# Even-layer attention: the value product as three f32r passes on split probabilities

## The reference, cut to what matters

```
def dense_gqa(q, k, v):          # 8 query heads, 2 key/value heads, head width 64
    s = einsum(q, k) * HEAD_DIM ** -0.5
    p = softmax(s)               # latent rows see all 1280 keys, context rows the 256 context keys
    return einsum(p, v)
```

## Time and profile before

| | before |
|---|---|
| runs | 3541.65, 3556.89, 3560.44 us, median 3556.89 |
| profiled execution | 3537.79 us (span 3536.0 us) |
| mean granted clock of TensorE | 0.849 |
| PE, DVE, ACT, POOL busy over the span | 79%, 43%, 29%, 15% |
| stage `attend_even`, 540 to 1110 us | PE 483, DVE 213, ACT 186, POOL 87 us busy; clock 0.91 |

### The profile page before, as it was taken

How to read it: one execution, slowest core, us unless ns; L and a number is a source line. 1 busy time by engine, 2 the same in 40 slices (tenths; PEclk the granted TensorE clock), 3 DMA queues, 4 the chain that set the end, 5 groups by cost and what they waited for, 6 DMA issues and landing times. The chain is left out here.

```text
span 3536.0 us, 34120 instructions
## 1 busy us (share of the span) xinstructions
PE 2802.4 (79%) x11887; PEld 2084.4 (59%) x11888; DVE 1531.6 (43%) x2383; ACT 1011.4 (29%) x1342; POOL 523.6 (15%) x473
## 2 busy tenths in 40 slices
PE   8948988889893699999137875876899993799991
PEld 1126865556562588888136433766788883688780
DVE  0024555343333556556442733333333333566754
ACT  0012224323231445444111012213222220455640
POOL 0012320310112200000221001321210112100001
PEclk9979989989896799999668987995777676899995
DMA  9532113611104567764620003134101104668855
GB/s 362 211 88 71 39 57 132 220 33 48 54 27 147 179 248 264 264 221 172 250 89 18 0 24 105 36 94 97 43 30 50 47 27 147 219 217 330 309 214 208
DMA packets 241445, 476.78 MB, mean 135 GB/s; under 512 B 85133, under 2 KB 98427, under 8 KB 237212
## 3 DMA queue, kind: packets, MB, share of 16 engines
q1 hardware_dynamic: 172264, 361.56, 29.3%
q0 software_dynamic: 19248, 65.60, 5.1%
q10 hardware_dynamic: 49812, 48.03, 4.2%
HBM read 387.70 MB, written 87.45 MB: 134 GB/s over the span
## 5 line engine op out<-in xcount | busy, mean ns | idle before, releaser
L2456 DVE TENSOR_TENSOR ex_gu_lo<-mw_gu,ex_gu_hi 128x2048 fp32r<-128x2048 f32 x128 | 287.3, 2287 | 78.8 <-ACT ex_gu_hi L2376 78.8
L2376 ACT ACTIVATE ex_gu_hi<-mw_gu 128x2048 fp32r<-128x2048 f32 x128 | 237.6, 1911 | 107.7 <-DVE ex_y L2503 101.7
L181 PE MATMUL mod_acc<-mod_w,mod_sT 128*2 128x512 f32 x384 | 174.5, 618 | 22.4 <-DMA mod_w<-in_ada_w 11.9
L2044 PE MATMUL at_ps_o<-at_pT,at_v_one 128*128 128x512 f32 x336 | 182.8, 626 | 1.7 <-ACT at_pT L1824 1.7
L2534 PE MATMUL ex_ps_g<-ex_gu_hi,ex_xT_hi 128*128 128x512 f32 x408 | 169.7, 416 | 8.0 <-issue 4.8
L2534 PE MATMUL ex_ps_y<-ex_d_hi,ex_hT_hi 128*128 128x512 f32 x408 | 166.5, 408 | 9.1 <-DVE ex_d_lo L2456 7.7
L2456 DVE TENSOR_TENSOR ex_d_lo<-mw_d,ex_d_hi 128x2048 fp32r<-128x2048 f32 x64 | 143.8, 2288 | 53.4 <-ACT ex_d_hi L2376 53.4
L1824 ACT ACTIVATE at_pT<-at_ps_s 128x512 f32<-128x512 f32 x168 | 99.5, 595 | 228.9 <-PE at_ps_s L2037 228.5
L2534 PE MATMUL ex_ps_g<-ex_gu_lo,ex_xT_hi 128*128 128x512 f32 x408 | 164.5, 403 | 0.0
L2534 PE MATMUL ex_ps_g<-ex_gu_hi,ex_xT_lo 128*128 128x512 f32 x408 | 164.5, 403 | 0.0
L2534 PE MATMUL ex_ps_y<-ex_d_lo,ex_hT_hi 128*128 128x512 f32 x408 | 162.0, 397 | 0.0
(11 more groups left out here) (452 smaller groups left out, 6422.6 us busy)
## 6 DMA issues: line engine op xcount, KB each, us to landing
mw_gu<-in_moe_w_gate SPq DMA_DIRECT2D x32, 2048.0 KB, 10.5
mw_gu<-in_moe_w_up SPq DMA_DIRECT2D x32, 2048.0 KB, 15.4
mw_d<-in_moe_w_down SPq DMA_DIRECT2D x32, 2048.0 KB
mod_w<-in_ada_w SPq DMA_DIRECT2D x32, 1536.0 KB, 9.4
y_d<-ex_y ACTq DMA_DIRECT2D x51, 512.0 KB
y_d<-at_zero POOLq DMA_DIRECT2D x36, 512.0 KB, 5.0
x_d<-at_x SPq DMA_DIRECT2D x18, 512.0 KB, 2.6
co_x<-x_d SPq DMA_DIRECT2D x18, 512.0 KB, 6.4
```

Of the source, the lines that this page charges most:

```text
L181: mm = nc.tensor.matmul(acc[0:2, n, :], sT[:, i, :], w[i][:, n * 512:(n + 1) * 512], start=(i == 0), stop=(i == KD - 1))
L2044: nc.tensor.matmul(ps_o[g][:, :], v_one[:, kt, g:g + 2, :].rearrange("p a d -> p (a d)"), pT[u % 3][:, :], start=(u == plan.first[i, g]), ...
L2376: nc.scalar.activation(dst, src, ACT.Copy).then_inc(sem, 1)
L2456: sub = lambda dst, a, b, sem: nc.vector.tensor_tensor(dst, a, as_f32(b), ALU.subtract).then_inc(sem, 1)
```

## The change

The value product becomes three f32r products: lo(v) hi(p) + hi(v) hi(p) + hi(v) lo(p). `v_hi` and `v_lo` are made once. For the probabilities ACT runs the same Exp twice, once into the fp32 tile `pT` (two of them now, not three) and once, rounded, into `pT_hi`. POOL subtracts the two into `pT_lo`. PE waits for POOL (semaphore `p_ready`) before the third pass. ACT waits for POOL's subtraction of step u-2 before it writes `pT` again. The space comes from the tile of zeros, cut from 1024 to 64 columns: the DMA of zeros now reads it 16 times per row.

```diff
-        v_one = ph.sb("v_one", [P, NT, 3, HD])
+        v_hi = ph.sb("v_hi", [P, NT, 3, HD], F32R)
+        v_lo = ph.sb("v_lo", [P, NT, 3, HD], F32R)
-        pT = [ph.sb(f"pT{i}", [P, 512]) for i in range(3)]
+        pT = [ph.sb(f"pT{i}", [P, 512]) for i in range(2)]
+        pT_hi = [ph.sb(f"pT_hi{i}", [P, 512], F32R) for i in range(3)]
+        pT_lo = [ph.sb(f"pT_lo{i}", [P, 512], F32R) for i in range(3)]
-        zero = ph.sb("zero", [P, D])
+        zero = ph.sb("zero", [P, D // 16])
...
 ACT, scores:
+                        if u >= 2:
+                            act.wait_ge(S["p_ready"], u - 1)
                         if u >= 3:
                             act.wait_ge(S["valued"], u - 2)
-                        nc.scalar.activation(pT[u % 3][:, :], ps_s[u % 3][:, :], ACT.Exp).then_inc(S["exp_done"], 1)
+                        nc.scalar.activation(pT[u % 2][:, :], ps_s[u % 3][:, :], ACT.Exp)
+                        nc.scalar.activation(pT_hi[u % 3][:, :], ps_s[u % 3][:, :], ACT.Exp).then_inc(S["exp_done"], 1)
 POOL:
-                        pool.dma_start(k.y_d[zeroed * P:(zeroed + 1) * P, :], zero[:, :]).then_inc(S["zeroed"], 16)
+                        pool.dma_start(k.y_d[zeroed * P:(zeroed + 1) * P, :].rearrange("p (a b) -> p a b", a=16), bc(zero[:, :], 1, 16)).then_inc(S["zeroed"], 16)
+                    if what == 'scores':
+                        pool.wait_ge(S["exp_done"], i + 1)
+                        if i >= 3:
+                            pool.wait_ge(S["valued"], i - 2)
+                        nc.gpsimd.tensor_tensor(pT_lo[i % 3][:, :], pT[i % 2][:, :], as_f32(pT_hi[i % 3][:, :]), ALU.subtract
+                                                ).then_inc(S["p_ready"], 1)
 DVE, once:
+                dve.wait_ge(S["copied"], 2)
+                nc.vector.tensor_tensor(v_lo[:, :, 0:3:2, :], k.v0[:, :, :].rearrange("p t (g d) -> p t g d", g=2),
+                                        as_f32(v_hi[:, :, 0:3:2, :]), ALU.subtract).then_inc(S["v_rest"], 1)
 PE, values:
-                        nc.tensor.matmul(ps_o[g][:, :], v_one[:, kt, g:g + 2, :].rearrange("p a d -> p (a d)"), pT[u % 3][:, :],
-                                         start=(u == plan.first[i, g]), stop=(u == plan.last[i, g])).then_inc(S["valued"], 1)
+                        hi, lo = (v[:, kt, g:g + 2, :].rearrange("p a d -> p (a d)") for v in (v_hi, v_lo))
+                        nc.tensor.matmul(ps_o[g][:, :], lo, pT_hi[u % 3][:, :], start=(u == plan.first[i, g]), stop=False)
+                        nc.tensor.matmul(ps_o[g][:, :], hi, pT_hi[u % 3][:, :], start=False, stop=False)
+                        pe.wait_ge(S["p_ready"], u + 1)
+                        nc.tensor.matmul(ps_o[g][:, :], hi, pT_lo[u % 3][:, :], start=False, stop=(u == plan.last[i, g])
+                                         ).then_inc(S["valued"], 1)
```

More of the change, by code:

```diff
@@ L1728, in attend_even @@
         S = {n: ph.sem(n) for n in (
-            "q_in m_in x_in rows_in rows_ready rw_in rw_hi_done rw_ready ones_ready copied scored exp_done valued drained q_hi q_lo max_done "
+            "q_in m_in x_in rows_in rows_ready rw_in rw_hi_done rw_ready ones_ready copied scored exp_done p_hi p_ready v_rest valued drained q_hi q_lo max_done "
             "nmx_zero nmx_done shifted summed aT_ready a_hi a_lo m_hi g_full tmp_ready x_added x_stored sq_done ms_done rstd_done "
@@ L1811, in _ @@
                 nc.scalar.activation(k_one[0:HD, :, :], as_f32(k.k0_both[0:HD, :, :]), ACT.Copy)
-                nc.scalar.activation(v_one[:, :, 0:3:2, :], k.v0[:, :, :].rearrange("p t (g d) -> p t g d", g=2), ACT.Copy
+                nc.scalar.activation(v_hi[:, :, 0:3:2, :], k.v0[:, :, :].rearrange("p t (g d) -> p t g d", g=2), ACT.Copy
                                      ).then_inc(S["copied"], 1)
@@ L1868, in _ @@
                 nc.gpsimd.memset(nmx[:, :], 0.0).then_inc(S["nmx_zero"], 1)
-                nc.gpsimd.memset(v_one[:, :, 1, :], 1.0).then_inc(S["ones_ready"], 1)
+                nc.gpsimd.memset(as_f32(v_hi[:, :, 1, :]), 1.0).then_inc(S["ones_ready"], 1)
+                nc.gpsimd.memset(as_f32(v_lo[:, :, 1, :]), 0.0).then_inc(S["ones_ready"], 1)
                 nc.gpsimd.memset(zero[:, :], 0.0).then_inc(S["zero_ready"], 1)
@@ L1998, in split_product @@
                     return mm
-                pe.wait_ge(S["ones_ready"], 1)
+                pe.wait_ge(S["ones_ready"], 2)
+                pe.wait_ge(S["v_rest"], 1)
                 for ev in plan.events:
```

## The result

| | before | after |
|---|---|---|
| median (range) of four runs each | 3549.27 (3540.74 to 3560.44) | 3609.06 (3605.08 to 3618.74) |
| profiled execution, span | 3536.0 us | 3617.0 us |
| clock over the span | 0.849 | 0.836 |

The ratio is 1.0171, 95% interval 1.0129 to 1.0212: 60 us slower. The forecast was 3608. The profiled execution of after is the slowest of its four, so its trace shows about 10 us more than the median; that of before is 12 us under its median. So the two traces are 81 us apart and not 60: 72 in the stage, 9 in code that didn't change.

A forecast was written before the change was run, and what follows sets the result against it. PE was taken to set the pace inside a tile, with a saving of at most about 30 us. Tiles +34, port +5 and zeros +12 made +51 us on 3557, so 3608 us; range 3550 to 3700.

The forecast's parts named there:

- (a): Tile boundary: two subtractions queued on POOL delay the third pass, so the output product starts later; +1.8 us a tile.
- (b): Between the two output products: POOL falls back but catches up, and PE keeps three steps' savings; -0.5 us a tile.
- (c): Second output product to h transposes: POOL's queue delays PE; +2.5 us, or +4.6 where few maximum blocks stand.
- After the transposes: Rest of a latent tile: the router gives POOL time and four steps save 0.17 us each; -0.8 us.
- Context tiles: The context tiles, 4 steps in 55 us: +1.5 us each for the boundary, +3 together.
- Tile 0: First tile, paced by weight pieces: 0.6 us more ACT work per step costs 0 to 10 us, taken as +4.
- The port: DVE instructions with two SBUF operands and POOL's work cost each other time; +5 us, bounds 0 and 20.
- The zeros: 36 issues of zeros, 0.53 us each, now lie in POOL's critical queue in two tiles; +12 us.
- the rival: Issuing zeros in pieces costs POOL: 3650 at 2 us an issue, 3720 at 4, about 3890 at 8.5; chance 0.20.
- the saving that arrives: Rival: PE stays the pace and POOL's lag is always hidden, giving 3532 us; chance 0.08.
- Three passes as slow as fp32: Rival: the three passes take as long as the fp32 product; no separate chance, inside break-even and the forecast.
- Break-even: Rival: lags are about half those walked, +17 us for the tiles, few zeros' issues on the path; 3550 to 3575, chance 0.17.

The follow-up runs named there:

- e1: Changed kernel without the low half of the probabilities: one Exp, no subtraction, third pass reads the high half again; 3532.27 us, ratio 0.995.
- e9: Changed kernel plus unread passes in the tile-boundary gaps and before step 15's third pass in latent tiles before a context tile and the last; 3598.92 us, ratio 1.0149.
- e10: Kernel before the change, plus unread filler passes on PE at the tile boundary and nothing else; 3540.19 us, ratio 0.9988.
- e2: Changed kernel without the subtraction; the second Exp stays but nobody reads its output, third pass reads the high half; 3546.87 us, ratio 0.9994.
- e4: Changed kernel with the 36 transfers of zeros issued by SyncE, four per tile, in place of GpSimd; 3601.35 us, ratio 1.0144.
- e6: Kernel before the change with only the zeros changed: 64 columns repeated 16 times, issued by GpSimd; 3553.41 us, ratio 1.0005.
- e5: Changed kernel without the low half of the probabilities (as e1), plus unread filler passes in the tile-boundary gaps; 3526.36 us, ratio 0.9938.
- e3: Changed kernel without the plain Exp: GpSimd subtracts the high half from itself, with the same PE waits for it; 3580.20 us, ratio 1.0088.

## Why the prediction came out right, and where its steps were off

- What bounds the kernel: right. PE's saving is 0.17 us a step at full clock (24 us found of 25). The ceiling of 30 us was wrong as a time: e1 got 16. The sum treated the clock as fixed at 0.91. This matters more for the loss.
- (a) boundary, +1.8 us: in latent tile 5 1.7 by the queue, and 1.3 more by the clock. In tiles 3, 4 and 6, with 24 blocks, it was wrong: with the gap filled, so at the full clock, the output product begins 11.0 us after the reciprocal in e9 and 11.1 in e10. GpSimd's queue adds nothing there; the walk took one boundary for both kinds of tile.
- (b) between the products, -0.5: 883.12 to 892.90 was 9.8 us, 933.09 to 942.56 is 9.5, so -0.3. The product ahead of it, 6.0 us before, took 7.2 because its first passes were at 1.2 GHz.
- (c) +4.6 in a tile with few blocks: 15.7 us against 11.1, exact, but partly by luck. The subtraction of step 14 ended 10.3 us into the stretch (walked 11.6), then POOL waited 1.16 us for VectorE's h, which the walk had as done meanwhile. (The stretch of the earlier trace rows is 12.96 us from 840.81, not 13.2: the product's last pass starts at 840.58.) In tiles 3, 4 and 6 it grew from 13.0 to 15.9, 18.0 and 16.7 us (17.1 in all three in e9), where 15.5 was walked. So with the clock kept up the tile sum of +3.0 came out right in latent tile 4 (58.5 us in e9, 55.5 in e10), out of terms that were each wrong: 0 for (a) in place of +1.8, +4.1 for (c) in place of +2.5.
- After the transposes -0.8: wrong, +3.4 (16.96 us against 13.55 to the next reciprocal), since the transposes and passes behind the wait of 3.17 us run at half clock. In e9, with that gap filled, it is -0.3.
- So tiles 5 and 7 lost 12 us each, not 5.1; in e9 tile 5 lost 6.8. This is the step that was mis-sized most: the clock behind a wait, taken as fixed. Latent tiles 3, 4 and 6 lost 3.3, 6.0 and 5.0, walked 3.0.
- Context tiles +1.5 each: wrong in sign, 1.2 and 1.3 us shorter. They run at 0.75, and e1, with no wait for POOL, has the same 1.4 and 1.7: four steps of 0.17 us are 0.7 us at 2.4 GHz and 1.4 at 1.2, and four steps give POOL no queue.
- Tile 0 +4: +6.4 to its reciprocal; e1 alone has +3.9 there (51.7 us at clock 0.86 against 47.8 at 0.96), so it is clock more than the second Exp; e2, which has that Exp too, is level with e1 there (+3.7).
- The port, +5 (0 to 20): VectorE's h and weight pieces took 19.8 - 12.8 = 7.0 and 17.1 - 11.1 = 6.0 us more. On the path lies the 1.16 us that POOL waits for h ahead of L1908, 10.0 us in 8 tiles by its line's waits. Within the bounds, near 10.
- The zeros, +12: 8 in the median of e4, 18 in its trace. The mechanism (issues ahead of subtractions in tiles 1 and 2) was right; the price was 1.24 us, not 0.53. The pieces do cost, 0.7 us an issue, near the low bound and under the 2 us at which the rival began. The transfer didn't become 2048 packets a time: the queue has 19248 packets before and after.
- The sum of +51 met the +60 to +73 that were found (median, and profiled stage with tile 0) because the median before fell 8 us in the newer runs while the loss was larger. 3608 against 3609 is closer than the working deserves, and part of it is luck. The forecast has 51 us net of the 29 saved, so 80 us of waits and lost savings; the stage showed 47 us of waits and some 54 of slower TensorE. The waits were too dear, the clock was missing, and the two errors nearly cancel.
- The rivals: the saving that arrives needs the subtraction of step 15 ready about 12 us into stretch (c); it was ready after about 15. Three passes as slow as fp32 is refuted by the pitch. Break-even is excluded by the interval.

What stays open: the low stretches were predicted by no step. The runs show that a filled boundary gap keeps the clock up behind it, not what decides whether it falls behind an open one. How the 60 us divide between waits and clock is known only roughly: busy and idle time of the stage put some 54 us on the clock, the table 49 of 67 (its full-clock sum grew by only 18, but it counts waits at the low clock as half), and the fillers of e9 gave back 10 in the median and 20 in the trace.

## What to carry to other kernels

Before work is moved from the busiest engine to an idle one, write down the idle one's queue in order for one period: a mean load of half says nothing when the consumer waits for the last item. Cost the helper's wait twice, once as the wait and once as the slower TensorE behind it. And a saving on TensorE itself is worth its cycles only if the clock stays: price it from a run with the saving alone before building the rest.

## What the runs showed of the hardware

- Cutting work from a busy TensorE lowered its granted clock, from 0.92 to 0.89 over nine tiles, and of 29 us saved at full clock only 16 arrived (e1); the gaps at its tile boundaries were at most 0.3 us longer, but for one of 0.5. In the tiles with 24 blocks the clock fell behind 13 of 16 such gaps (before, e6, e1, after), and behind none of 12 that were filled with unread passes (e5, e9, e10).
- An issue by GpSimd of a transfer whose source is read 16 times per row takes 1.22 us, against 0.53 for one run per row, though the record has the same number of packets (19248 on that queue in both).
- GpSimd and VectorE slow each other: 2.28 us in place of 1.28 for a two-operand instruction of 128x1024, 1.75 in place of 0.75 for a `tensor_scalar`, and up to 2.26 in place of 1.28 for the subtraction beside two of VectorE's.
- A GpSimd subtraction of a tile from itself took 1.04 us, of one tile from another 1.28 (medians of 168, e3 and after).
